# A hybrid decoder step on one core: the decode samples' softmax and value products are moved from a stage of their own into the heads of the prompt attention

## The reference, cut to what matters

```
k_past, v_past = cache_k[page_table], cache_v[page_table]    # 8 samples x 1024 tokens x 2 kv heads x 128
att = q . k * 128 ** -0.5 over the selected tokens and the new one      # 8 heads, 4 to a kv head
p   = softmax(att)
o   = p_past @ v_past + p_new * v_new
x   = x + concat(o) @ w_out1, then the MLP
```

## Time and profile before

| | |
|---|---|
| three runs | 2888.82, 2890.40, 2890.56 us, median 2890.4 |
| profiled execution | 2892.67 us, span 2890.5 us |
| mean granted TensorE clock | 0.934 |
| busy: PE, DVE, ACT, POOL | 2696.4, 1194.2, 573.7, 969.3 us |
| prompt attention | 1786.8 to 1962.5 us |
| samples' stage | 1962.8 to 2031.1 us |

### The profile page before, as it was taken

How to read it: one execution, slowest core, us unless ns; L and a number is a source line. 1 busy time by engine, 2 the same in 40 slices (tenths; PEclk the granted TensorE clock), 3 DMA queues, 4 the chain that set the end, 5 groups by cost and what they waited for, 6 DMA issues and landing times. The chain is left out here.

```text
span 2890.5 us, 42505 instructions
## 1 busy us (share of the span) xinstructions
PE 2696.4 (93%) x16417; PEld 2568.6 (89%) x16417; DVE 1194.2 (41%) x2409; ACT 573.7 (20%) x1043; POOL 969.3 (34%) x420
## 2 busy tenths in 40 slices
PE   8899867899999999999878998998999999999998
PEld 7798756799999999999847997777999999999998
DVE  6959355353112121135358974751453122121223
ACT  3010143212001010011034533540211010010112
POOL 4323301235445344444302311000344444444442
PEclk9999978799999999999978986995899999999998
DMA  6534433311111111111212223003311111111111
GB/s 195 103 78 91 114 95 88 121 44 44 51 44 44 51 44 44 51 44 43 91 29 81 86 69 117 1 1 117 102 39 49 44 51 45 44 51 44 44 51 66
DMA packets 291409, 188.41 MB, mean 65 GB/s; under 512 B 41030, under 2 KB 281290, under 8 KB 290522
## 3 DMA queue, kind: packets, MB, share of 16 engines
q1 hardware_dynamic: 262518, 173.56, 19.9%
q10 hardware_dynamic: 28772, 13.30, 3.0%
HBM read 151.84 MB, written 34.98 MB: 65 GB/s over the span
## 5 line engine op out<-in xcount | busy, mean ns | idle before, releaser
L390 POOL TENSOR_TENSOR w_hi<-w_raw,ones 128x1024 fp32r<-128x1024 f32 x180 | 435.3, 2419 | 1622.8 <-PE ps L399 1481.6
L392 POOL TENSOR_TENSOR w_lo<-w_raw,w_hi 128x1024 fp32r<-128x1024 f32 x180 | 500.9, 2783 | 25.9 <-issue 0.4
L399 PE MATMUL ps<-next_hi,w_hi 128*128 128x344 f32 x1920 | 420.5, 328 | 13.5 <-PEq L1924 9.0
L399 PE MATMUL ps<-out_x_hi,w_hi 128*128 128x344 f32 x1920 | 409.3, 322 | 8.1 <-DVE out_x_lo L1961 8.1
L399 PE MATMUL ps<-next_lo,w_hi 128*128 128x344 f32 x1920 | 413.2, 324 | 0.0
L399 PE MATMUL ps<-next_hi,w_lo 128*128 128x344 f32 x1920 | 410.7, 323 | 0.0
L399 PE MATMUL ps<-out_x_lo,w_hi 128*128 128x344 f32 x1920 | 409.1, 321 | 0.0
L399 PE MATMUL ps<-out_x_hi,w_lo 128*128 128x344 f32 x1920 | 406.9, 320 | 0.0
L1986 DVE TENSOR_TENSOR resid<-ps,resid 128x344 f32 (+1 forms) x240 | 108.8, 509 | 649.1 <-PE ps L399 649.1
L399 PEld LDWEIGHTS ps<-next_hi,w_hi 128*128 128x128 f32 x1920 | 329.5, 192 | 15.3 <-issue 14.3
L399 PEld LDWEIGHTS ps<-out_x_hi,w_hi 128*128 128x128 f32 x1920 | 324.7, 189 | 8.2 <-issue 8.2
(11 more groups left out here) (541 smaller groups left out, 2901.4 us busy)
## 6 DMA issues: line engine op xcount, KB each, us to landing
w_raw<-in_w_up SPq DMA_DIRECT2D x64, 512.0 KB, 4.0
w_raw<-in_w_down SPq DMA_DIRECT2D x64, 512.0 KB, 4.1
w_raw<-in_w_in SPq DMA_DIRECT2D x36, 512.0 KB, 4.7
resid_spill<-resid SPq DMA_DIRECT2D x2, 4128.0 KB, 14.4
ml_inputs<-in_ring SPq DMA_DIRECT2D x16, 516.0 KB, 3.0
resid<-resid_spill SPq DMA_DIRECT2D x4, 2064.0 KB, 7.3
w_raw<-in_w_out SPq DMA_DIRECT2D x16, 512.0 KB, 4.3
resid<-ml_inputs SPq DMA_DIRECT2D x8, 1024.0 KB, 8.4
```

Source lines behind the costliest of these rows:

```text
L390: m.nc.gpsimd.tensor_tensor(parts(hi), x, one, ALU.mult)
L392: return m.nc.gpsimd.tensor_tensor(parts(lo), x, hi, ALU.subtract)
L399: ins = nc.tensor.matmul(out[c], parts(w), parts(x[:, token_cols(c)]), start=first and n == 0, stop=last and n == 2)
```

## The change

`phase_attend_samples` is dropped. Its work is written into `phase_attend`:

- VectorE makes the first maximum after `mask(0)` and `mask(1)`. The further steps stand after `norm(n)` or in it for n = 0, 2, 7, 8 and 60, ScalarE's two exponentials at its n = 5, TensorE's small products in front of the values of heads 0, 2 and 8.
- The value products are 16 tasks, one for a sample and kv head, in front of the values of heads 12, 15, 18, ... 57.
- The small results and the sums lie in other columns of the bank that holds a head's output.
- All pages are fetched by SP, in the order of the samples, into four buffers: two in rows of `m.proj`, one in `resid`, one in `keys`. Samples 4 to 7 wait for sample b - 4's products; the wait for the stores stands before sample 3.

```diff
+    smp_at = {12 + 3 * t: (t // KVH, t % KVH) for t in range(B * KVH)}
+    top_at, spread_at, exp_at, add_at, sum_at, out_at = 0, 2, 5, 7, 8, 60
@@ sync
-            sp.wait_ge(m.stored.sem, m.stored.at(6 * 16))
+            for b in range(B):
+                if b == 3:
+                    sp.wait_ge(m.stored.sem, m.stored.at(6 * 16))
+                for j in range(PAGES):
+                    page = sp.value_load(s.table[0:1, b * PAGES + j:b * PAGES + j + 1], min_val=0, max_val=last_page)
+                    if j == 0 and b >= 4:
+                        sp.wait_ge(m.pe_e.sem, m.pe_e.at(b - 3))
+                    sp.dma_start(v_pages[b % 4][j], m.ins["cache_v"][bass.ds(page, 1)].rearrange("a p h d -> p (a h d)")
+                                 ).then_inc(m.page_in[b].sem, 16)
@@ tensor, called in values(n) after its waits and before its products
+            def sample_task(n):
+                if n == top_at:
+                    pe.wait_ge(m.dve_d.sem, m.dve_d.at(1))
+                    nc.tensor.transpose(top_row, flat3(s.top), m.ident[:])
+                if n == spread_at:
+                    pe.wait_ge(m.dve_d.sem, m.dve_d.at(2))
+                    nc.tensor.matmul(top_all, m.ones[0:BH, :], s.top_d, start=True, stop=True)
+                if n == sum_at:
+                    pe.wait_ge(m.dve_d.sem, m.dve_d.at(4))
+                    nc.tensor.matmul(sum_all, m.ones[:], flat3(s.total), start=True, stop=True)
+                if n in smp_at:
+                    b, g = smp_at[n]
+                    pe.wait_ge(m.dve_d.sem, m.dve_d.at(5))
+                    pe.wait_ge(m.page_in[b].sem, m.page_in[b].at(16 * PAGES))
+                    at = b * AH + g * AG
+                    for j in range(PAGES):
+                        last = nc.tensor.matmul(o_smp[:, at:at + AG], v_pages[b % 4][j][:, g * DH:(g + 1) * DH],
+                                                s.s_logit[:, j, b, g * AG:(g + 1) * AG], start=(j == 0), stop=(j == PAGES - 1))
+                    if g == KVH - 1:
+                        last.then_inc(m.pe_e.sem, 1)
@@ vector, in norm(n) before its signal
+                if n == top_at:
+                    ins = V.reduce_max(s.top_t[:, 0:1], top_row, AX_X)
+                if n == spread_at:
+                    ins = V.tensor_tensor(flat3(s.top), top_all, flat3(s.new_logit), ALU.max)
+                if n == sum_at:
+                    ins = V.tensor_tensor(flat3(s.total), sum_all, flat3(s.new_p), ALU.add)
+                if n == out_at:
+                    ins = V.tensor_tensor(m.normed[:, :, T:N], o_smp.rearrange("p (b h) -> p h b", b=B),
+                                          s.new_p.rearrange("p b h -> p h b"), ALU.add)
@@ vector, sample_part(n) after norm(n)
+                if n == spread_at:
+                    V.drain()
+                    V.tensor_tensor(by_j, by_j, flat3(s.top).unsqueeze(1).to_broadcast([P, PAGES, BH]), ALU.subtract)
+                    V.tensor_tensor(s.new_p, s.new_logit, s.top, ALU.subtract).then_inc(m.dve_d.sem, 1)
+                if n == add_at:
+                    dve.wait_ge(m.act_d.sem, m.act_d.at(1))
+                    V.reduce_sum(flat3(s.total), s.s_logit.rearrange("p j b h -> p (b h) j"), AX_X).then_inc(m.dve_d.sem, 1)
...
@@ scalar, at the end of the loop's body
+                if n == exp_at:
+                    act.wait_ge(m.dve_d.sem, m.dve_d.at(3))
+                    nc.scalar.activation(flat4, flat4, ACT.Exp, scale=scale)
+                    nc.scalar.activation(flat3(s.new_p), flat3(s.new_p), ACT.Exp, scale=scale).then_inc(m.act_d.sem, 1)
...
-          phase_in1, phase_rows, phase_index, phase_topk, phase_attend, phase_attend_samples,
+          phase_in1, phase_rows, phase_index, phase_topk, phase_attend,
```

More of the change, by code:

```diff
@@ L3001, in phase_attend @@
     n_heads = len(heads)
+    quarters = lambda rows: [m.proj[:, row, p * KVH * DH:(p + 1) * KVH * DH] for row in rows for p in range(PAGES // 2)]
+    spare = r.take(PAGES, KVH * DH)
+    old_keys = Carver(m.keys[:, :, TB * KVH * DH:]).take(PAGES, KVH * DH)
+    v_pages = [quarters((0, 1)), quarters((VT1, VT1 + 1)), [spare[:, j] for j in range(PAGES)],
+               [old_keys[:, j] for j in range(PAGES)]]
+    BH = B * AH
+    flat3 = lambda t: t.rearrange("p b h -> p (b h)")
+    flat4 = s.s_logit.rearrange("p j b h -> p (j b h)")
+    by_j = s.s_logit.rearrange("p j b h -> p j (b h)")
+    last_page = m.ins["cache_v"].shape[0] - 1
+    top_row, top_all, sum_all, o_smp = ps_o[0:BH, DH:DH + P], ps_o[:, 256:256 + BH], ps_o[:, 320:320 + BH], ps_o[:, 384:384 + BH]
+    top_at, spread_at, exp_at, add_at, sum_at, out_at = 0, 2, 5, 7, 8, 60
+    smp_at = {12 + 3 * t: (t // KVH, t % KVH) for t in range(B * KVH)}
     def dve_blocks(i):
@@ L3047, in values @@
                     pe.wait_ge(m.dve_c.sem, m.dve_c.at(n))
+                sample_task(n)
                 for b in range(i + 1):
@@ L3103, in norm @@
                 V.drain()
-                V.tensor_scalar(o_tok[n % 2], ps_o[:, 0:DH], st[:, a + 3:a + 4], None, ALU.mult).then_inc(m.dve_c.sem, 1)
+                ins = V.tensor_scalar(o_tok[n % 2], ps_o[:, 0:DH], st[:, a + 3:a + 4], None, ALU.mult)
+                if n == top_at:
[4 more added lines that the diff above has]
+                    ins = V.tensor_tensor(flat3(s.total), sum_all, flat3(s.new_p), ALU.add)
@@ new lines, in norm, with sample_part @@
+                if n == out_at:
+                    ins = V.tensor_tensor(m.normed[:, :, T:N], o_smp.rearrange("p (b h) -> p h b", b=B),
+                                          s.new_p.rearrange("p b h -> p h b"), ALU.add)
+                ins.then_inc(m.dve_c.sem, 1)
+            def sample_part(n):
+                if n == top_at:
+                    V.drain()
+                    V.tensor_scalar(s.top_d, m.ident[0:BH, 0:BH], s.top_t[:, 0:1], None, ALU.mult).then_inc(m.dve_d.sem, 1)
+                if n == spread_at:
+                    V.drain()
+                    V.tensor_tensor(by_j, by_j, flat3(s.top).unsqueeze(1).to_broadcast([P, PAGES, BH]), ALU.subtract)
[3 more added lines that the diff above has]
+                    V.reduce_sum(flat3(s.total), s.s_logit.rearrange("p j b h -> p (b h) j"), AX_X).then_inc(m.dve_d.sem, 1)
+                if n == sum_at:
+                    V.drain()
+                    V.reciprocal(s.total, s.total)
+                    V.drain()
+                    V.tensor_tensor(by_j, by_j, flat3(s.total).unsqueeze(1).to_broadcast([P, PAGES, BH]), ALU.mult
+                                    ).then_inc(m.dve_d.sem, 1)
+                    V.tensor_tensor(s.new_p, s.new_p, s.total, ALU.mult)
+                    V.drain()
+                    for g in range(KVH):
+                        part = slice(g * AG, (g + 1) * AG)
+                        V.tensor_tensor(s.new_p[:, :, part], s.new_p[:, :, part],
+                                        x[:, VT1 + g, T:N].unsqueeze(2).to_broadcast([P, B, AG]), ALU.mult)
+                    V.drain()
@@ L3106, in _ @@
             mask(0)
             mask(1)
+            V.tensor_reduce(flat3(s.top), s.s_logit.rearrange("p j b h -> p (b h) j"), AX_X, ALU.max).then_inc(m.dve_d.sem, 1)
             for n in range(n_heads + 1):
@@ L3114, in _ @@
                     norm(n - 1)
+                    sample_part(n - 1)
         @block.scalar
@@ L3148, in _ @@
                     out(n - 2)
+                if n == exp_at:
+                    act.wait_ge(m.dve_d.sem, m.dve_d.at(3))
+                    nc.scalar.activation(flat4, flat4, ACT.Exp, scale=scale)
+                    nc.scalar.activation(flat3(s.new_p), flat3(s.new_p), ACT.Exp, scale=scale).then_inc(m.act_d.sem, 1)
     for q in (m.pe_a, m.pe_b, m.pe_c, m.pe_d, m.act_a, m.act_b, m.act_c, m.dve_a, m.dve_b, m.dve_c):
         q.passed(n_heads)
+    m.pe_e.passed(B)
+    m.dve_d.passed(5)
+    m.act_d.passed(1)
+    for q in m.page_in:
+        q.passed(16 * PAGES)
     m.dma_a.passed(16)
@@ L3154, in phase_attend @@
     m.stored.passed(6 * 16)
[L3157 to L3252, removed]
```

## The result

The changed kernel's first four runs have a median of 2855.44 us against 2889.61 us before, a ratio of 0.9889 with a 95% interval of 0.9862 to 0.9916. One of the four took 6605.88 us, which no other execution comes near; the ratio leaves it out, and the other three are 2850.90, 2851.07 and 2859.80. Five further runs beside nine of the kernel before gave 2850.12 against 2885.48 us, a ratio of **0.9877 (0.9852 to 0.9901)**, 35.4 us less; the first comparison gives 34.2. The forecast was 30.2 us less, 2860.2, with a range of 2849 to 2873.

What follows compares the result with a forecast made beforehand. TensorE, by its work and its waits, was taken to set the time. Terms -68.55 + 28.4 + 6.3 + 4.8 - 1.2 = -30.2 us, from the median of 2890.4 to 2860.2 us; range 2849 to 2873.

Steps and rivals of the forecast that it cites:

- The stage removed: Decode samples' own stage after the prompt attention, its edge included, goes whole from the path: -68.55 us.
- The products: 16 value-product tasks added to heads 12 to 57, 1.80 us each at full clock, little hidden: +28.4 us.
- The softmax: VectorE and ScalarE work added to heads 0 to 8, where VectorE is in the chain: +6.3 us, lower bound 0.9.
- The clock falls: TensorE's clock falling behind task bursts, mostly in blocks 1 and 2: 3 falls of 1.6 us, +4.8 us.
- The projection behind: Output projection after the attention starts with less time at half clock: -1.2 us, at most 2.5 to be had.
- The pages: All 64 page fetches on SP's queue land before the heads that need them: cost 0.
- that of no falls: Rival: no clock fall in the prompt attention and softmax mostly hidden at 2 us; -40.7, 2849.7 us; chance 0.22.
- That of a fall at nearly every task: Rival: clock falls behind nearly all 16 tasks in the heads, 25.6 us; -8.3, 2882.1 us; chance 0.16.
- The slow side: Rival: clock does not come back between bursts over heads 12 to 57; +97, 2987 us; chance 0.04.

Runs made afterwards that it cites:

- one product: Changed kernel with each task making one of its eight products, the other seven pages fetched but not multiplied: 2827.88 us, against 2891.12 for the kernel before.
- the second trace: The changed kernel profiled once more, nothing edited; its runs gave 2850.12 us against 2885.48 for the kernel before, loop 206.5 us.
- double bursts: Two edits of the changed kernel: tasks placed two at a time, 2859.70 us; every task's eight products made twice at the same places, 2909.58 us.
- the last one: Changed kernel with eight tasks (samples 4 to 7) in one piece before the last head's values: 2863.17 us, against 2891.12 for the kernel before.

## Why the prediction was right

- **The stage removed**, 68.55 us: right to a tenth. The projection starts 1.3 us behind the last normalisation, as the samples' stage did.
- **The products**, forecast 28.4, measured 28.6. The price from the selection stage held, at full clock and not at the half clock of the stage they came from. The 0.4 us that block 1 was to hide did not show.
- **The softmax**, forecast 6.3 for the engines' work alone. That work costs 4.8 us and 0.3 ahead of head 0; 1.9 more come from a start that stays longer at half clock. The sum, 7.0, is near, but by luck: its parts are not those of the forecast, which had no term for the start. The lower bound of 0.9 was too low as well, for it counted VectorE's idle time in all of block 1, of which only head 8 carries softmax. Of the six traces with the softmax in the first heads, four have the long start (nine intervals of 18.4 to 19.1 us, clock 0.70 to 0.77) and two don't (17.2 us, 0.94 and 0.95, with every product twice and with one product), although these heads run the same code in all; with the softmax later, in two traces, it is not there. That the softmax brings it about is likely, but not shown.
- **The clock falls**, forecast 4.8 us for three: none came behind a task, in either trace. This is the term that failed. The one fall of the second trace stands in heads 9 to 11, ahead of the first task, and cost 1.2 us. The four falls in seven rounds of the selection stage were a fair count for that stage (eight of the nine traces have four, one has two), but were read as the rate of a burst anywhere. There eight transposes followed each burst; here a burst stands between score and value products. No run took the transposes away, so that they make the difference is an argument. The runs with double bursts show that such falls do come among dense products, at twice the length.
- **The projection behind**, forecast 1.2, measured 1.5: its stretch is at 0.87, before at 0.72.
- **The pages**, forecast 0: no wait for them in the trace.

Sum: -68.55 + 28.6 + 7.0 + 0.4 - 1.5 = -34.05, where 0.4 is what remains of the loop's 35.7. The forecast of -30.2 is 3.9 short, and the falls that did not come are 4.8.

Of the rivals, that of no falls had that part right and forecast 2 us for the softmax, which cost 7.0; its -40.7 us promises 5.3 to 6.5 us more than the medians show, the forecast's -30.2 promises 4.0 to 5.2 less. By the time alone the two could hardly be told apart; the clock in the stretches with tasks and the nine intervals tell them apart. That of a fall at nearly every task did not come; the kernels with double bursts go that way. The slow side did not come, but the kernel with every product twice shows what stands behind it: 63 us at half clock.

The Trainium skill, "TensorE: Matmul & The Clock Gate", Part 1, lets the gate follow how busy the engine has been. The result agrees with what that gives for single bursts, but the reason isn't gaplessness: in the run with two tasks at a time TensorE was busy 133.1 of 134 us and lost 10.7 us to the clock, and in the last one it went to 0.50 without a gap.

## What to carry to other kernels

Products with 4 moving columns in a stage of their own ran at the slow clock here; woven into dense work in short pieces they cost half, 0.22 us instead of 0.43 a product. The pieces have to be short: the same work in pieces twice as long gave back 10.6 of the 35 us. Small work for other engines belongs into the heads where TensorE is the bound, not into the first ones where those engines are in the chain (here 4.6 to 5.2 us of the loop, with the slow start).

Before a gain is read from two profiles, compare a point ahead of the change: 7.2 of the 41.3 us between the two spans had passed before the changed stage began.

## What was not expected of the hardware

That busy TensorE and its clock come apart so sharply: 16 records of 4-column products in a row cost no clock, 32 in a row cost 1.3 us a burst on average (10.6 us over eight) in blocks where everything else is dense. And that the length of the slow start changes between executions of the same heads: over the same code the clock was 0.70 in one trace and 0.95 in another, worth 1.9 us.
